# Matrix memory on one Trainium2 core: scores from stacked rounded halves, and another order of the steps of each head

## The chip, the cores and the metric

The kernel runs on one core of one Trainium2 chip. The metric is the device time of one execution in microseconds (us). Five engines work side by side, each through a list of instructions in order, and wait for each other on semaphores: TensorE (PE in the profile, its weight loads PEld), VectorE (DVE), ScalarE (ACT), GpSimd (POOL) and the DMA queue's issuer SyncE (SP).

## What is computed

The program runs three transformer layers over 512 latent and 256 context tokens of width 1024. The change lies in the second layer's mixer, a matrix memory (mLSTM) with 8 heads, keys and queries 64 wide and values 128 wide. For the last layer that needs only the latents, the reference's chunked scan equals, for each head, direction and query token t, a weighted sum over the keys s that t may see:

```python
s = jnp.einsum('bhtd,bhsd->bhts', qc, kc) * jnp.exp(logw - m_t[..., None])
num = w_inter[..., None] * jnp.einsum('bhvd,bhtd->bhtv', C, qc) + jnp.einsum('bhts,bhsv->bhtv', s, vc)
den = w_inter * jnp.einsum('bhd,bhtd->bht', n, qc) + jnp.sum(s, axis=-1)
h = num / jnp.maximum(jnp.abs(den), jnp.exp(-m_t))[..., None]
```

The forward and the backward result are added, normed over the 128 value columns (rmsnorm), multiplied by a gain and by a sigmoid gate, and go into the output projection.

## The kernel before, in words

The stage is `mlstm_stage` (lines 3052 to 3332), called once by `mix1`. It does not run the scan: it forms, for each head h and each of six 128-key blocks (`order` = 4, 5, 0, 1, 2, 3; 4 and 5 are the context), the score product of all 512 queries, and multiplies it by decay weights for both directions. The steps of a head, with their engine and line:

- **staging** (POOL, L3107): the head's 64 rows of queries are copied into one half of `qS`, the other 64 rows of which are zero, because `kT` holds two heads' keys in 128 rows. Two buffers, by parity of h.
- **spread_tops** (PE, L3120): two products put the running maxima of the two directions on all partitions of PSUM.
- **open_corners** (DVE, L3262): eight 128x128 instructions write the exponents of the diagonal blocks into `prob`.
- **weigh** 0 to 5 and **weigh_corners** (ACT, L3196, L3201): exponentials of the rest, and of the corners.
- **score** 0 to 5 (PE, L3131): one product in f32, which shows as two matmul passes. Score j waits until mix j-2 has read its PSUM bank.
- **mix** 0 to 5 (DVE, L3249): the score times the weight, for each direction, into `prob`.
- **weighted_sums** 0 to 2 (PE, L3146): 36 products in f32, two passes each (24, 30 and 18 records), of `prob` with the values and a column of ones, which gives the divisor too.
- **divisors** (DVE, L3274 to L3281), **read_first** (ACT, L3207) and **add_second** (DVE, L3287): divide and add the two directions into `hs`.
- **root** (ACT, L3214 to L3218): four sums of squares, a table load, Ln, a table load, Exp.
- **norm_heads** (DVE, L3294), **turn** (PE, L3155, four transposes), **put_out** (DVE, L3301).

The order is written by hand for each engine, as a loop over h in which three heads are in flight: head h is scored and mixed, head h-1 summed, divided and added, head h-2 normed and turned, and ACT weighs head h+1. In one turn of the loop the engines do before the change:

- PE: score 0, 1; sums 0 of h-1; score 2; sums 1 of h-1; turn h-2; score 3; spread_tops h+1; sums 2 of h-1; score 4, 5.
- ACT: weigh 0, 1 of h+1; read_first h-1; corners and weigh 2 of h+1; root h-1; weigh 3, 4, 5 of h+1.
- DVE: mix 0, 1, 2; norm h-2; mix 3; put_out h-2; open_corners h+1; mix 4, 5; divisors and add_second of h-1.
- POOL: staging, for which it waits until all scores of head h-2 are done.

The first weighted sums of a head wait for three of the four read_first of the head before (`first_read`), the others for add_second (`added`). The last head's divisors, root and norm are done by `LastHead` beside the projection that follows, and are not changed. Context for the costs: elsewhere the kernel multiplies f32 data as rounded halves of type fp32r (high, and the rest as low), one pass each.

Of the kernel before, what the change touches and what calls it, by code (L numbers as in the profile page):

```python
# [13 lines left out]
F32 = mybir.dt.float32  # L14
# [6 lines left out]
P = 128  # L21
# [103 lines left out]
class Kernel:  # L125


    def __init__(self, nc, arrays, stack):
# [66 lines left out]
        self.norm_high = sem("norm_high")  # L195
        self.norm_low = sem("norm_low")
        self.tail_lat = sem("tail_lat")
        self.last_divided = sem("last_divided")
        self.last_read = sem("last_read")
        self.last_added = sem("last_added")  # L200
# [2848 lines left out]
HEADS = 8  # L3049


def mlstm_stage(K, qT, kT, keysT, floorT, top, val, sig, yT):
# [20 lines left out]
    hs = lambda t: K.xT[:, t // 2, LAT + P * (t % 2):LAT + P * (t % 2) + P]  # L3073
    with ExitStack() as stack:
        sb = lambda name, shape: stack.enter_context(K.temp(name, shape))
        qS = sb("qS", [P, 2, LAT])
        prob = sb("prob", [P, 2, 2, 6 * LAT])
        hn, junk = sb("hn", [P, 4, P]), sb("junk", [P, P])
        den, ss = sb("den", [P, 2, 4]), sb("ss", [P, 4])
# [12 lines left out]
        @block.gpsimd  # L3092
        def _(pool):
            chain = Chain(pool, K.pool_chain)
            for half in range(2):
                r = slice(64 * half, 64 * half + 64)
                chain.step(nc.gpsimd.tensor_copy(both[r, :], K.ident[r, r]))
            chain.sync()
            for b in range(2):
                chain.step(nc.gpsimd.memset(qS[64 - 64 * b:128 - 64 * b, b, :], 0.0))  # L3100
            chain.sync()
            for h in range(HEADS):
                b, r = h % 2, slice(64 * (h % 2), 64 * (h % 2) + 64)
                if h >= 2:

                    pool.wait_ge(scored.sem, scored.base + JOBS * (h - 1))
                nc.gpsimd.tensor_copy(qS[r, b, :], qT[r, h // 2, :]).then_inc(staged.sem, 1)  # L3107
            chain.close()

        @block.tensor  # L3110
        def _(pe):
            def spread_tops(h):
                if h == 0:
                    pe.wait_ge(staged.sem, staged.base + 1)
                else:

                    pe.wait_ge(weighed.sem, weighed.base + JOBS * h)
                for d in range(2):
                    row = 32 * d + h
                    mm = nc.tensor.matmul(tops(d, 0, LAT), both[:, row:row + 1].broadcast_to([P, P]), top[:],  # L3120
                                          start=True, stop=True)
                mm.then_inc(spread.sem, 1)

            def score(h, j):
                g, s = JOBS * h + j, order[j]
                if j == 0:
                    pe.wait_ge(staged.sem, staged.base + h + 1)
                if g >= 2:

                    pe.wait_ge(mixed.sem, mixed.base + g - 1)  # L3130
                nc.tensor.matmul(scores(g), kT[:, h // 2, s * P:s * P + P], qS[:, h % 2, :],  # L3131
                                 start=True, stop=True).then_inc(scored.sem, 1)

            def weighted_sums(h, n):
                if n == 0:
                    pe.wait_ge(mixed.sem, mixed.base + JOBS * h + JOBS)
                if h > 0:

                    if n == 0:
                        pe.wait_ge(first_read.sem, first_read.base + 4 * h - 1)  # L3140
                    else:
                        pe.wait_ge(added.sem, added.base + 4 * h - (1 if n == 1 else 0))
                for d, t in (((0, 0), (0, 1), (0, 2)), ((1, 0), (1, 1), (1, 2)), ((0, 3), (1, 3)))[n]:
                    keys = [4, 5] + (list(range(t + 1)) if d == 0 else list(range(t, 4)))
                    for m, s in enumerate(keys):
                        mm = nc.tensor.matmul(K.psum[:, sums(d, t):sums(d, t) + 129], weight(h, d, s, t * P, t * P + P),  # L3146
                                              val[:, s, h, :], start=m == 0, stop=m == len(keys) - 1)
                mm.then_inc(summed.sem, 1)

            def turn(h):  # L3150
                pe.wait_ge(normed.sem, normed.base + h + 1)
                if h > 0:
                    pe.wait_ge(out_ready.sem, out_ready.base + h)
                for t in range(4):
                    mm = nc.tensor.transpose(turns[:, t * P:t * P + P], hn[:, t, :], K.ident[:])  # L3155
                mm.then_inc(turned.sem, 1)

            spread_tops(0)
            for h in range(HEADS + 1):
                now, one_back, two_back = h < HEADS, 1 <= h <= HEADS, h >= 2  # L3160
                if now:
                    score(h, 0)
                    score(h, 1)
                if h == HEADS:
                    pe.wait_ge(out_ready.sem, out_ready.base + h - 2)
                    K.keep_busy(turns, 8)
                if one_back:
                    weighted_sums(h - 1, 0)
                if now:
                    score(h, 2)  # L3170
                if one_back:
                    weighted_sums(h - 1, 1)
                if two_back:
                    turn(h - 2)
                if now:
                    score(h, 3)
                if h + 1 < HEADS:
                    spread_tops(h + 1)
                if one_back:
                    weighted_sums(h - 1, 2)  # L3180
                if now:
                    score(h, 4)
                    score(h, 5)

        @block.scalar
        def _(act):
            def weigh(h, j):
                s = order[j]
                if j == 0:

                    act.wait_ge(diag_ready.sem, diag_ready.base + h + 1)
                for d in range(2):
                    lo, hi = beyond(s, d)
                    if hi > lo:
                        col = 32 * d + h
                        op = nc.scalar.activation(weight(h, d, s, lo, hi), tops(d, lo, hi), ACT.Exp,  # L3196
                                                  bias=keysT[:, s, col:col + 1], scale=-1.0)
                op.then_inc(weighed.sem, 1)
# [4 lines left out]
            def read_first(h):  # L3203

                act.wait_ge(den_ready.sem, den_ready.base + h + 1)
                for t in range(4):
                    nc.scalar.activation(hs(t), K.psum[:, sums(0, t):sums(0, t) + P], ACT.Identity,  # L3207
                                         scale=den[:, 0, t:t + 1]).then_inc(first_read.sem, 1)

            def root(h):  # L3210
# [7 lines left out]
                nc.scalar.activation(ss[:], ss[:], ACT.Exp, scale=-0.5).then_inc(rooted.sem, 1)  # L3218
                chain.close()

            for h in range(-1, HEADS):
                ahead, back = h + 1 < HEADS, h >= 1
                if ahead:
                    weigh(h + 1, 0)
                    weigh(h + 1, 1)
                if back:
                    read_first(h - 1)
                if ahead:
                    weigh_corners(h + 1)
                    weigh(h + 1, 2)  # L3230
                if back:
                    root(h - 1)
                if ahead:
                    for j in range(3, JOBS):
                        weigh(h + 1, j)

            nc.scalar.activation(K.root[:], K.eps[:], ACT.Sqrt)

# [1 line left out]
        def _(dve):  # L3240
# [58 lines left out]
            def put_out(h):  # L3299
                dve.wait_ge(turned.sem, turned.base + h + 1)  # L3300
                nc.vector.scalar_tensor_tensor(yT[:, h, 0:LAT], turns, K.v("out_g", h), sig[:, h, :],  # L3301
                                               ALU.mult, ALU.mult).then_inc(out_ready.sem, 1)

            dve.wait_ge(K.loaded.sem, K.loaded.base + 16)
            open_corners(0)
            for h in range(HEADS + 1):
                now, one_back, two_back = h < HEADS, 1 <= h < HEADS, h >= 2
                if now:
                    mix(h, 0)
                    mix(h, 1)  # L3310
                    mix(h, 2)
                if two_back:
                    norm_heads(h - 2)
                if now:
                    mix(h, 3)
                if two_back:
                    put_out(h - 2)
                if h + 1 < HEADS:
                    open_corners(h + 1)
                if now:  # L3320
                    mix(h, 4)
                    mix(h, 5)
                if one_back:
                    divisors(h - 1)
                    add_second(h - 1)
            chain.close()
    K.loaded.base += 16
    for c, n in ((spread, HEADS), (scored, JOBS * HEADS), (summed, 3 * HEADS), (turned, HEADS - 1),
                 (weighed, JOBS * HEADS), (rooted, HEADS - 1), (first_read, 4 * HEADS - 4), (mixed, JOBS * HEADS),
                 (den_ready, HEADS - 1), (added, 4 * HEADS - 4), (normed, HEADS - 1), (diag_ready, HEADS),  # L3330
                 (out_ready, HEADS - 1), (staged, HEADS)):
        c.base += n


# [945 lines left out]
```

## Time and profile before

| | us |
|---|---|
| median of 3 runs | 2786.57 (2785.32 to 2791.9) |
| the profiled execution's own time | 2783.43 |
| its span in the trace | 2781.7 |
| busy in the span: PE, PEld | 2661.6, 2163.9 |
| busy in the span: DVE, ACT, POOL | 1515.0, 914.2, 285.5 |

The span goes from the first to the last instruction. Times of a row are in us from the start of the span unless marked ns. A row of the timeline merges neighbouring instructions of one kind: start, time from the first start to the last end, engine, line, operation, output and inputs, shape and count, and in brackets how long the engine was idle before and whose signal ended that. The end of an instruction overlaps the start of the next by a pipeline's depth, so the cost of one in a row of many is the distance of the starts. The stage of the change lies between 1360.5 and 1501.3 us.

### The profile page before, as it was taken

Reading aid. Unit: us, or ns where it says so; the run is one execution under the profiler, and the core shown is the slowest. Engines: PE = TensorE matmul, PEld = TensorE weight load, DVE = VectorE, ACT = ScalarE, POOL = GpSimd, SP = SyncE. Lnnn points to the kernel's source line nnn. Section 1 sums busy time; section 2 is a strip of 40 time slices with the busy share of each in tenths; the row PEclk is TensorE's granted clock in tenths of the full one; section 3 lists DMA queues with packets and bytes.
Section 4 is the critical chain, followed back from the end, with each engine's and each line's share of the span. In section 5 each row is a group of like instructions: output and inputs, shape, how many; then the busy total and the mean of one; then the engine's idle time right before and its main releaser. Section 6 shows DMA issues by size and latency. Waiting matters only on the chain. (4 is left out here: it accounts for less than half of the span.)

```text
span 2781.7 us, 32433 instructions
## 1 busy us (share of the span) xinstructions
PE 2661.6 (96%) x13424; PEld 2163.9 (78%) x13424; DVE 1515.0 (54%) x2047; ACT 914.2 (33%) x1222; POOL 285.5 (10%) x161
## 2 busy tenths in 40 slices
PE   7998999999999999999889999999999899999998
PEld 5876666688888888888767888888686678888887
DVE  6326899874329536571366543444789833433332
ACT  4332434423212212352265331332323622332221
POOL 2111223000000000000000000000240644000000
PEclk9999999999999999999999999999999999999999
DMA  7011001331125324122001222223120222222221
GB/s 273 25 51 54 31 31 46 145 136 68 62 75 204 144 79 171 46 93 89 18 1 46 83 80 102 106 73 110 61 86 14 77 105 91 76 97 93 106 82 62
DMA packets 37037, 236.10 MB, mean 85 GB/s; under 512 B 4128, under 2 KB 5152, under 8 KB 13216
## 3 DMA queue, kind: packets, MB, share of 16 engines
q1 hardware_dynamic: 36896, 234.11, 23.4%
q8 instruction: 103, 1.69, 0.2%
q14 instruction: 38, 0.31, 0.0%
HBM read 231.99 MB, written 2.10 MB: 84 GB/s over the span
## 5 line engine op out<-in xcount | busy, mean ns | idle before, releaser
L369 PE MATMUL pair<-h_high,w_high 128*128 128x512 f32 x1984 | 714.4, 369 | 10.2 <-DVEq L1239 4.9
L370 PE MATMUL pair<-h_low,w_high 128*128 128x512 f32 x1984 | 710.1, 366 | 0.0
L375 PE MATMUL pair<-h_high,w_low 128*128 128x512 f32 x1984 | 444.4, 366 | 0.8 <-POOL w_low L323 0.8
L323 DVE TENSOR_TENSOR w_low<-ring,w_high 128x2048 fp32r<-128x2048 f32 (+5 forms) x164 | 342.1, 2091 | 186.4 <-ACT w_high L301 178.9
L369 PEld LDWEIGHTS pair<-h_high,w_high 128*128 128x128 f32 x1984 | 374.1, 189 | 76.2 <-issue 7.3
L370 PEld LDWEIGHTS pair<-h_low,w_high 128*128 128x128 f32 x1984 | 374.3, 189 | 64.0 <-issue 1.4
L375 PEld LDWEIGHTS pair<-h_high,w_low 128*128 128x128 f32 x1984 | 346.1, 189 | 63.0 <-POOL w_low L323 1.2
L301 ACT ACTIVATE w_high<-ring 128x2048 fp32r<-128x2048 f32 (+4 forms) x166 | 288.1, 1736 | 309.4 <-PE pair L375 203.9
L369 PE MATMUL pair<-high,w_high 128*128 128x512 f32 (+1 forms) x704 | 249.1, 363 | 1.0 <-DVE low L1283 1.0
L370 PE MATMUL pair<-low,w_high 128*128 128x512 f32 (+1 forms) x704 | 249.0, 363 | 0.0
L1275 DVE TENSOR_TENSOR gate<-gate,pair 128x512 f32<-128x512 f32 (+1 forms) x66 | 51.2, 776 | 239.0 <-PE pair L375 230.1
L311 POOL CAST w_high<-ring 128x1024 fp32r<-128x1024 f32 x25 | 30.5, 1249 | 1299.3 <-DVE coef L724 706.1
L375 PE MATMUL pair<-high,w_low 128*128 128x512 f32 (+1 forms) x704 | 153.8, 363 | 0.0
L369 PEld LDWEIGHTS pair<-high,w_high 128*128 128x128 f32 x704 | 132.8, 189 | 22.8 <-DVE low L1283 2.1
L370 PEld LDWEIGHTS pair<-low,w_high 128*128 128x128 f32 x704 | 132.9, 189 | 20.8
L375 PEld LDWEIGHTS pair<-high,w_low 128*128 128x128 f32 x704 | 122.0, 189 | 20.6
L1224 ACT ACTIVATE high<-gate 128x512 fp32r<-128x512 f32 (+2 forms) x66 | 46.4, 704 | 277.7 <-DVE gate L1275 277.7
L323 POOL TENSOR_TENSOR w_low<-ring,w_high 128x2048 fp32r<-128x2048 f32 x21 | 97.1, 4624 | 111.0 <-ACT w_high L301 110.4
L2097 ACT ACTIVATE prob<-pair 128x512 f32<-128x512 f32 x112 | 65.0, 594 | 122.8 <-PE pair L2038 122.6
L2051 PE MATMUL pair<-prob,val 128*128 128x512 f32 x192 | 99.1, 598 | 0.0
L1111 DVE SCALAR_TENSOR_TENSOR xT<-pair,mod,xT 128x512 f32<-128x512 f32 (+1 forms) x48 | 27.5, 613 | 106.9 <-PE pair L375 106.9
L1215 ACT ACTIVATE gate<-pair,vec 128x768 f32<-128x768 f32 (+1 forms) x44 | 38.9, 884 | 132.6 <-PE pair L375 119.5
(464 smaller groups left out, 4011.4 us busy)
## 6 DMA issues: line engine op xcount, KB each, us to landing
ring<-in_w_up SPq DMA_DIRECT2D x66, 1024.0 KB, 4.8
ring<-in_w_ada SPq DMA_DIRECT2D x32, 1024.0 KB, 4.8
ring<-in_w_down SPq DMA_DIRECT2D x32, 704.0 KB, 4.0
ring<-in_w_ada0r SPq DMA_DIRECT2D x16, 1024.0 KB, 4.8
ring<-in_w_merge_b SPq DMA_DIRECT2D x14, 1024.0 KB, 4.8
ring<-in_w_down SPq DMA_DIRECT2D x8, 1024.0 KB, 4.7
ring<-in_w_att_in SPq DMA_DIRECT2D x6, 1024.0 KB, 5.2
ring<-in_w_heads SPq DMA_DIRECT2D x6, 1024.0 KB, 5.0
```

Of the source, the lines that this page charges most:

```text
L301: self.nc.scalar.activation(self.w_high[:, n % 2, 0:floats], self.ring[:, chunk % RING, 0:floats], ACT.Copy).then_inc(self.high_ready.sem, 1)
L311: return engine.tensor_copy(to, of)
L323: (on or self.nc.vector).tensor_tensor(self.w_low[:, n % 2, 0:floats], self.ring[:, chunk % RING, 0:floats], self.w_high[:, n % 2, 0:float ...
L369: self.nc.tensor.matmul(out[:, a:e], w_high[:, k, at], high[:, k, a:e], start=k == 0, stop=False)
L370: self.nc.tensor.matmul(out[:, a:e], w_high[:, k, at], low[:, k, a:e], start=False, stop=False)
L375: mm = self.nc.tensor.matmul(out[:, a:e], w_low[:, k, at], high[:, k, a:e], start=False, stop=k == kt - 1)
L1111: op = nc.vector.scalar_tensor_tensor(x, self.out(b)[:, a:e], K.mod[:, self.gate * KD + b, a // LAT:a // LAT + 1], x, ALU.mult, ALU.add)
L1215: nc.scalar.activation(g, ps[:, 0:tokens], ACT.Identity, bias=bias, scale=middle).then_inc(tap_ready.sem, 1)
L1224: nc.scalar.activation(one(high[:, bass.ds(i * RING + s, 1), 0:tokens]), g, ACT.Copy).then_inc(high_done.sem, 1)
L1275: nc.vector.tensor_tensor(g[:, 0:tokens], g[:, 0:tokens], K.pairs[2 * (s % 2) + 1][:, 0:tokens], ALU.mult).then_inc(hidden_ready.sem, 1)
L2051: mm = nc.tensor.matmul(out_lat(u), values(u, s), prob[:, g % 3, :], start=s == 0, stop=s == 5)
L2097: nc.scalar.activation(prob[:, g % 3, :], scores(g), ACT.Exp).then_inc(exped.sem, 1)
```

## The change

1. **Scores.** `kS` holds, for each parity, the rounded (fp32r) keys of the head in its own 64 rows and the rest, keys minus rounded keys, in the other 64; `qS` holds the rounded queries in both halves; `qL` the rest of the queries. A score is then two fp32r products: `kS` with `qS` over 128 rows, and the head's rows of `kS` with `qL` over 64. The product of the two rests is left out. (`qS` in the other half is written from `qT` and rounded on the way.)
2. **Staging.** POOL does five operations a head in place of one (three copies, two subtractions). Head 0 is staged by ACT (two copies) and DVE (one copy, two subtractions), ahead of their loops; PE's first score waits for that. The two memsets go.
3. **Order.** PE: scores 4 and 5 stand ahead of sums 2 of h-1. ACT: read_first h-1 stands first, then weigh 0 and 1, corners, weigh 2 to 5 of h+1, and root h-1 last. DVE: after put_out come mix 4, 5, divisors h-1, then open_corners h+1, then add_second h-1.

```diff
@@ staging
-        qS = sb("qS", [P, 2, LAT])
+        half = lambda name, shape: stack.enter_context(K.temp(name, shape, F32R))
+        kS, qS, qL = half("kS", [P, 2, ALL]), half("qS", [P, 2, LAT]), half("qL", [P, LAT])
+        own = lambda h: slice(64 * (h % 2), 64 * (h % 2) + 64)
+        other = lambda h: own(h + 1)
...
-            for half in range(2):
-                r = slice(64 * half, 64 * half + 64)
-                chain.step(nc.gpsimd.tensor_copy(both[r, :], K.ident[r, r]))
-            chain.sync()
-            for b in range(2):
-                chain.step(nc.gpsimd.memset(qS[64 - 64 * b:128 - 64 * b, b, :], 0.0))
-            chain.sync()
-            for h in range(HEADS):
-                b, r = h % 2, slice(64 * (h % 2), 64 * (h % 2) + 64)
+            nc.gpsimd.tensor_copy(both[0:64, :], K.ident[0:64, 0:64])
+            nc.gpsimd.tensor_copy(both[64:P, :], K.ident[64:P, 64:P]).then_inc(staged.sem, 1)
+            for h in range(1, HEADS):
+                b, r, o = h % 2, own(h), other(h)
                 if h >= 2:
                     pool.wait_ge(scored.sem, scored.base + JOBS * (h - 1))
-                nc.gpsimd.tensor_copy(qS[r, b, :], qT[r, h // 2, :]).then_inc(staged.sem, 1)
+                chain.step(nc.gpsimd.tensor_copy(qS[r, b, :], qT[r, h // 2, :]))
+                chain.step(nc.gpsimd.tensor_copy(kS[r, b, :], kT[r, h // 2, :]))
+                nc.gpsimd.tensor_copy(qS[o, b, :], qT[r, h // 2, :])
+                chain.sync()
+                nc.gpsimd.tensor_tensor(qL[r, :], qT[r, h // 2, :], qS[r, b, :].bitcast(F32), ALU.subtract)
+                nc.gpsimd.tensor_tensor(kS[o, b, :], kT[r, h // 2, :], kS[r, b, :].bitcast(F32),
+                                        ALU.subtract).then_inc(staged.sem, 1)
@@ score, and the loop of TensorE
-                if j == 0:
+                if j == 0 and h == 0:
+                    pe.wait_ge(K.head_low.sem, K.head_low.base + 1)
+                elif j == 0:
                     pe.wait_ge(staged.sem, staged.base + h + 1)
...
-                nc.tensor.matmul(scores(g), kT[:, h // 2, s * P:s * P + P], qS[:, h % 2, :],
-                                 start=True, stop=True).then_inc(scored.sem, 1)
+                b, keys = h % 2, slice(s * P, s * P + P)
+                nc.tensor.matmul(scores(g), kS[:, b, keys], qS[:, b, :], start=True, stop=False)
+                nc.tensor.matmul(scores(g), kS[own(h), b, keys], qL[own(h), :],
+                                 start=False, stop=True).then_inc(scored.sem, 1)
...
-                if one_back:
-                    weighted_sums(h - 1, 2)
                 if now:
                     score(h, 4)
                     score(h, 5)
+                if one_back:
+                    weighted_sums(h - 1, 2)
@@ ScalarE
+            nc.scalar.activation(qS[own(0), 0, :], qT[own(0), 0, :], ACT.Copy).then_inc(K.head_high.sem, 1)
+            nc.scalar.activation(kS[own(0), 0, :], kT[own(0), 0, :], ACT.Copy).then_inc(K.head_high.sem, 1)
             for h in range(-1, HEADS):
                 ahead, back = h + 1 < HEADS, h >= 1
+                if back:
+                    read_first(h - 1)
                 if ahead:
                     weigh(h + 1, 0)
                     weigh(h + 1, 1)
-                if back:
-                    read_first(h - 1)
-                if ahead:
                     weigh_corners(h + 1)
-                    weigh(h + 1, 2)
+                    for j in range(2, JOBS):
+                        weigh(h + 1, j)
                 if back:
                     root(h - 1)
-                if ahead:
-                    for j in range(3, JOBS):
-                        weigh(h + 1, j)
@@ VectorE
+            r, o = own(0), other(0)
+            dve.wait_ge(K.head_high.sem, K.head_high.base + 1)
+            nc.vector.tensor_copy(qS[o, 0, :], qT[r, 0, :])
+            nc.vector.tensor_tensor(qL[r, :], qT[r, 0, :], qS[r, 0, :].bitcast(F32), ALU.subtract)
+            dve.wait_ge(K.head_high.sem, K.head_high.base + 2)
+            nc.vector.tensor_tensor(kS[o, 0, :], kT[r, 0, :], kS[r, 0, :].bitcast(F32),
+                                    ALU.subtract).then_inc(K.head_low.sem, 1)
...
-                if h + 1 < HEADS:
-                    open_corners(h + 1)
                 if now:
                     mix(h, 4)
                     mix(h, 5)
                 if one_back:
                     divisors(h - 1)
+                if h + 1 < HEADS:
+                    open_corners(h + 1)
+                if one_back:
                     add_second(h - 1)
```

## Rows read from the trace of the kernel before

**Rows 1.** The page's first part: busy time of each engine over the whole span.
```profile
PE 2661.6 (96%) x13424; PEld 2163.9 (78%) x13424; DVE 1515.0 (54%) x2047; ACT 914.2 (33%) x1222; POOL 285.5 (10%) x161
```

**Rows 2.** Windows: stretch, length, busy PE, PEld, DVE, ACT, POOL, granted clock, DMA.
```profile
1360.00:1362.00 2.00, 0.00 (x0) 0.00 (x0) 0.20 (x1) 1.28 (x1) 1.34 (x4) 1.00 0.24 61
...
1363.20:1366.50 3.30, 3.30 (x6) 1.32 (x4) 2.16 (x8) 0.28 (x1) 0.31 (x1) 0.50 0.00 0
1366.60:1369.90 3.30, 1.37 (x3) 0.30 (x2) 2.30 (x4) 3.30 (x6) 0.00 (x0) 1.00 0.00 0
...
1374.00:1490.00 116.00, 102.95 (x632) 77.07 (x631) 74.08 (x207) 72.42 (x173) 3.66 (x6) 1.00 0.00 1
```

**Rows 3.** Timeline of TensorE in one turn (h = 5) of the loop.
```profile
1444.02 2.92 PE L3146 MATMUL pair<-val,prob 128*128 128x129 f32 x24 [0.47 <-ACT xT L3207]
...
1447.64 3.51 PE L3146 MATMUL pair<-val,prob 128*128 128x129 f32 x30
...
1451.54 1.02 PE L3131 MATMUL pair<-qS,kT 128*128 128x512 f32 x2
...
1452.87 2.17 PE L3146 MATMUL pair<-val,prob 128*128 128x129 f32 x18
```

**Rows 4.** Timeline of VectorE in the same turn.
```profile
1442.16 0.22 DVE L3274 SCALAR_TENSOR_TENSOR den<-pair,floorT 128x6 f32<-128x6 f32 x2
...
1442.68 0.20 DVE L3281 RECIPROCAL den<-den 128x8 f32<-128x8 f32 x1
...
1450.30 0.69 DVE L3294 TENSOR_TENSOR hn<-xT,ss 128x512 f32<-128x512 f32 x1 [1.58 <-ACT ss L3218]
1452.60 0.89 DVE L3249 SCALAR_TENSOR_TENSOR prob<-pair,prob 128x384 f32<-128x384 f32 x2 [1.61 <-PE pair L3131]
1453.41 0.74 DVE L3301 SCALAR_TENSOR_TENSOR yT<-pair,vec,sig 128x512 f32<-128x512 f32 x1
1455.16 2.16 DVE L3262 SCALAR_TENSOR_TENSOR prob<-pair,keysT,causal 128x128 f32<-128x128 f32 x8 [1.01 <-PE pair L3146]
1457.24 1.67 DVE L3249 SCALAR_TENSOR_TENSOR prob<-pair,prob 128x256 f32<-128x256 f32 x4
```

**Rows 5.** Timeline of ScalarE in the same turn, up to the next one's first weighing.
```profile
1440.69 2.42 ACT L3196 ACTIVATE prob<-pair,keysT 128x512 f32<-128x512 f32 x4 [5.37 <-DVE prob L3262]
1442.98 1.15 ACT L3207 ACTIVATE xT<-pair,den 128x128 f32<-128x128 f32 x4
1443.98 1.10 ACT L3201 ACTIVATE prob<-prob 128x1024 f32<-128x1024 f32 x1
...
1445.39 0.36 ACT L3214 ACTIVATE junk<-xT 128x128 f32<-128x128 f32 x1
...
1447.16 1.28 ACT L3216 ACT_TABLE_LOAD   x1
...
1450.18 1.81 ACT L3196 ACTIVATE prob<-pair,keysT 128x256 f32<-128x256 f32 x5
1457.35 2.42 ACT L3196 ACTIVATE prob<-pair,keysT 128x512 f32<-128x512 f32 x4 [5.37 <-DVE prob L3262]
```

**Rows 6.** Timeline of TensorE: two fp32r products, one after the other.
```profile
1503.31 0.39 PE L1375 MATMUL pair<-h_low,w_high 128*128 128x512 f32 x1
...
1503.54 0.40 PE L1375 MATMUL pair<-h_high,w_high 128*128 128x512 f32 x1
```

**Rows 7.** Timeline around 2284, VectorE then GpSimd, and one GpSimd line's durations (ns min/median/max).
```profile
2284.24 4.23 DVE L3936 TENSOR_TENSOR cc<-cc,hd 128x512 f32<-128x512 f32 x1
...
2283.28 4.64 POOL L323 TENSOR_TENSOR w_low<-ring,w_high 128x2048 fp32r<-128x2048 f32 x1 [6.62 <-ACT w_high L301]
...
L2206 POOL TENSOR_TENSOR c_low<-xT,c_high x8: 1812/1831/2808, 275.7 to 374.3; 64x768 fp32r<-64x768 f32 x8
```

**Rows 8.** Timeline of the stage's first corners and of its last sums.
```profile
1364.03 2.16 DVE L3262 SCALAR_TENSOR_TENSOR prob<-pair,keysT,causal 128x128 f32<-128x128 f32 x8 [3.83 <-PE pair L3120]
...
1498.80 2.17 PE L3146 MATMUL pair<-val,prob 128*128 128x129 f32 x18
```

More of the change, by code:

```diff
@@ L197, in __init__ @@
         self.tail_lat = sem("tail_lat")
+        self.head_high = sem("head_high")
+        self.head_low = sem("head_low")
         self.last_divided = sem("last_divided")
@@ L3330, in mlstm_stage @@
                  (den_ready, HEADS - 1), (added, 4 * HEADS - 4), (normed, HEADS - 1), (diag_ready, HEADS),
-                 (out_ready, HEADS - 1), (staged, HEADS)):
+                 (out_ready, HEADS - 1), (staged, HEADS), (K.head_high, 2), (K.head_low, 1)):
         c.base += n
```

## The prediction, made before the changed kernel was run

> **What bounds the kernel now.** The page puts TensorE at 2661.6 of 2781.7 us busy [rows 1], so I first asked whether the stage of the change is bound by it as well. The windows say: 102.95 of 116 us busy between 1374 and 1490, at a granted clock of 1.00 [rows 2]. That leaves over a tenth idle, so work taken from TensorE is not simply time saved. I therefore followed one turn of the loop (h = 5) through the timelines, and every wait in it. ScalarE's first weighings of two turns start at 1440.69 and 1457.35 [rows 5]: a turn takes 16.66 us. Two closed chains compete for that.
>
> *Chain A, through the sums.* Sums 0 start at 1444.02 when ScalarE's read_first is done; sums 1 and 2 follow with scores and transposes between them, and what waits for the end of sums 2 is open_corners, at 1455.16 [rows 3, 4]. Corners take 2.16, ScalarE then weighs for 2.29 (1440.69 to 1442.98) and reads for some 1.0 before the next sums 0 [rows 5]: 11.14 + 2.19 + 2.29 + 1.04 = 16.66. This chain binds.
>
> *Chain B, through the root.* ScalarE: weigh 2.29, read 1.00, corners and weigh 2 1.41, then the root; norm_heads starts at 1450.30, so the root costs 1450.30 - 1445.39 = 4.91 [rows 4, 5]. Then norm 0.69, transposes and start of score 3 0.55 (1450.99 to 1451.54), score 3 until mix 3 1.06, mix 3 0.81, put_out 0.74, after which VectorE stood 1.01 idle for sums 2 [rows 3, 4], then corners 2.16 + 0.03. Without that idle time the chain is 15.65 us. So chain B has 1.0 us of slack, no more. What is to be seen: norm_heads of head h-2 stands before mix 3 of head h in VectorE's list, so all that stands behind it waits for ScalarE's root.
>
> **Part 1, the scores.** An f32 score is two passes, 1.02 us to its end [rows 3]; two fp32r products follow each other at 0.23 and the last ends 0.40 after its start [rows 6]. A score costs TensorE 0.46 for some 0.86, 2.4 us per head. On chain B only score 3 counts: 1.06 becomes 0.23 + 0.40 + 0.04 = 0.67. That the second product has 64 rows is taken to gain nothing; a gain would be at most 0.23.
>
> **Part 2, staging.** GpSimd's dearest step is a 64x768 subtraction, 1.83 us median [rows 7]; five steps of at most that are under 9.2 us, my estimate is 5.2. It starts when head h-2 is scored and is due a whole turn later: hidden by head h-1's turn of 16.7 us, costed at nothing. Were that cover gone, the whole 5.2 would stand ahead of each head's score 0. Beside it VectorE does instructions with one operand in PSUM, for which I take nothing.
> At the head of the stage it does matter. VectorE must copy and subtract twice after ScalarE's first copy, about 0.6 + 0.7 + 1.0 from 1361.1 on (a 128x512 instruction of this kind takes 0.69, [rows 4]): first corners at 1363.4, where they were at 1364.03 [rows 8]. But GpSimd stages head 1 in that time, and a VectorE tensor_tensor on 128x512 took 4.23 us when a GpSimd subtraction had started 0.96 before it, ending 0.55 after that one [rows 7]. If both subtractions are held until GpSimd's chain of 5.2 is through, corners start at 1367.4. I take 1364.8, nearer to the lower end since most of GpSimd's steps there are short.
> The Trainium skill (GPSIMD Engine Reference, Key points) says that the two engines share their SBUF interfaces and contend when the VectorE instruction has two SBUF inputs. The trace agrees; by the rule alone the start is late, without it 0.6 us early.
>
> **Part 3, the order.** Chain A: scores 4 and 5 come ahead of sums 2, read_first no longer waits for corners and weighings. It becomes sums 0 2.76, score 2 0.46, sums 1 3.4, transposes 0.4, score 3, spread, scores 4 and 5 1.84, sums 2 2.29, divisors 0.72, three reads 0.95 [rows 3 to 6]: 12.8 us. It would bind no more.
> Chain B, from the moment R when a root is done: norm 0.69 and 0.55 as before, 0.67, so mix 3 starts at R+1.91 and ends its share at 2.72. Now put_out (0.74), mix 4 and 5 (about 1.6) stand ahead of the divisors: 5.05. On TensorE score 5 waits for mix 3 (2.85 with the signal), ends at 3.3, and sums 2, now behind it, take 2.29 from 3.35: 5.65. So the divisors start at 5.65, end 0.72 later (1442.16 to 1442.88), corners run from 6.45 to 8.61, weigh starts at R+8.65. ScalarE had nothing to do meanwhile but the read. Then weigh 0, 1 2.29, corners and weigh 2 1.41, weigh 3 to 5 some 1.64 (the row's 1.81 less the overlap), which used to come behind the root, and the root 4.91: 10.25 [rows 4, 5]. **Turn: 18.9 us**, where it was 16.66. Of the terms, the moved weighings give +1.64, mix 4 and 5, sums 2 and divisors ahead of corners +1.95, the read -1.00, the score -0.39. There are five such turns from the root of head 0 to that of head 5: +11.2.
> Start: head 0 has its own path. spread of head 1 waits for all of head 0's weighings (corners 2.16 + 5.34 after the first corners), and score 4 stands behind it, then mix 4 and 5, then corners of head 1; walked through by the same durations the first root is done 37.8 after the first corners, before 36.3 (1364.03 to 1400.3). +1.5, and +0.8 for the later corners: +2.3, between +0.9 and +4.9.
> Tail: from the root of head 5 (1483.6) to the last sums' end (1500.97, [rows 8]) it was 17.3. Now divisors end at 6.37, three reads at 7.2, sums 0 and 1 to 13.5, transposes and sums 2 16.1: -1.2.
>
> **The clock.** In the new turn TensorE is done with sums 1 at about R+15.1 (read 7.3, sums 0, score 2 behind mix 0 at 11.2, sums 1) and goes on at R+19.6: 4.5 us idle. In this trace the clock was 0.50 in 1363.2 to 1366.5, right after some 3 us of idleness (nothing in 1360 to 1362), again after a stretch with 1.37 of 3.3 us busy, and 1.00 all through the loop, where the longest pauses are 1.5 [rows 2]. So I expect the lower level, 1.2 GHz, once per head, over a stretch like those of the rows, most of it behind the pause. Then transposes (+0.4) and score 3 (+0.6) double and spread and score 4 keep score 5 back: +1.1 per turn and in the tail. Bounds: nothing, and +2.0 where it reaches into sums 2. 5.5 and 1.1.
> The Trainium skill (TensorE: Matmul & The Clock Gate, Why this matters for your kernels) warns of idle gaps between bursts of matmuls, as they bring the low rate back. That speaks against this change; without the rule its turn is 18.9, with it 20.
>
> **Sum.** 2.3 + 11.2 + 5.5 - 0.1 = +18.9, against the profiled execution's 2783.43: 2802.3. That execution lies 3.1 below the median of the runs, 2786.57, so the median forecast is 2805.
>
> **Rivals.** (a) *The clock holds at 2.4 GHz.* The pause falls where it does no harm, as the loop's 1.5 us pauses do now. 2.3 + 11.2 - 1.2 = +12.3: 2799. For: it has held for 116 us. Against: the new pause is three times as long.
> (b) *The clock falls for longer*, +2.0 a turn, and staging holds VectorE at the start: 4.9 + 11.2 + 10 + 0.8 = +27: 2813.
> (c) *Faster: the root stays off the path*, its place being VectorE's norm_heads. Chain A then sets the turn, 12.8, or ScalarE's own list, 11.3: 3.8 x 5 = -19, with start and tail -18: 2769. It decides when the chain through the root falls under 16.66, 2.2 us shorter than I make it. For: TensorE is the busiest engine and loses 2.4 us per head. Against: VectorE already idles 1.58 for the root [rows 4] though it comes earlier in ScalarE's list now.
> (d) *No difference.* The two table loads of the root (1.28 each, [rows 5]) disappear in the new order: turn 16.3, sum near -0.7: 2786. Against: Exp, Ln, Exp still alternate.
>
> **Chances.** Forecast 0.48, (a) 0.20, (b) 0.15, (c) 0.08, (d) 0.09. The range 2795 to 2814 holds the first three, with the bounds of the start. A measurement of this kernel can tell about 0.3%, 8.4 us, from no change: all of the first three are beyond it, so slower 0.83, same 0.09, faster 0.08.
>
> **What would show it.** First weighings of successive turns 19 to 20 us apart; VectorE's idle time before norm_heads up from 1.58 to some 5, ended by ScalarE's Exp; ScalarE idle some 7 between a root's end and the first weighing, the read within; TensorE idle some 4 before the transposes; score passes 0.23 apart; granted clock under 1.00 in the loop. I am wrong if turns are shorter than 16.7, if the wait before norm_heads is no longer than now, or if GpSimd's staging ends a wait of TensorE in the loop.

## The result, and the profile after

The changed kernel takes 2828.41 us (median of 4 runs, 2828.31 to 2829.63), the kernel before 2786.31 in the runs beside it: 1.0156 times as long, 95% interval 1.0144 to 1.0168. The profiled execution of after has a span of 2827.9 us, 46.2 more than before. The forecast was 2805 in a range of 2795 to 2814. The kernel did become slower, as forecast, but by 42.1 us where the sum had 18.9.

Nearly all of it lies in the stage of the change, which ends at 1545.8 us (GpSimd's first instruction of the next stage), before at 1501.3. By VectorE's norm_heads the 44.6 us divide like this: head 0's norm comes 7.0 later (1407.27 for 1400.31), the five turns from head 0's to head 5's take 34.4 more (117.7 for 83.3), the tail 3.2 more.

Timeline of VectorE in one turn of the kernel after; it answers to [rows 4]; the last row but one is ScalarE's first weighing. L3305 is norm_heads, L3260 the mixes, L3312 put_out, L3285 to L3292 the divisors, L3273 the corners.

```profile
1454.90 0.69 DVE L3305 TENSOR_TENSOR hn<-xT,ss 128x512 f32<-128x512 f32 x1 [5.48 <-ACT ss L3230]
1457.40 0.89 DVE L3260 SCALAR_TENSOR_TENSOR prob<-pair,prob 128x384 f32<-128x384 f32 x2 [1.82 <-PE pair L3143]
1458.21 0.74 DVE L3312 SCALAR_TENSOR_TENSOR yT<-pair,vec,sig 128x512 f32<-128x512 f32 x1
1459.70 0.89 DVE L3260 SCALAR_TENSOR_TENSOR prob<-pair,prob 128x256 f32<-128x256 f32 x2 [0.75 <-PE pair L3143]
1461.15 0.89 DVE L3260 SCALAR_TENSOR_TENSOR prob<-pair,prob 128x128 f32<-128x128 f32 x2 [0.56 <-PE pair L3143]
1465.32 0.23 DVE L3285 SCALAR_TENSOR_TENSOR den<-pair,floorT 128x6 f32<-128x6 f32 x2 [3.28 <-PE pair L3158]
...
1466.09 2.16 DVE L3273 SCALAR_TENSOR_TENSOR prob<-pair,keysT,causal 128x128 f32<-128x128 f32 x8
1468.29 2.42 ACT L3208 ACTIVATE prob<-pair,keysT 128x512 f32<-128x512 f32 x4 [1.05 <-DVE prob L3273]
...
1478.60 0.69 DVE L3305 TENSOR_TENSOR hn<-xT,ss 128x512 f32<-128x512 f32 x1 [5.48 <-ACT ss L3230]
```

The turn is 23.70 us. The idle time before norm_heads has gone from 1.58 to 5.48, as forecast. Count from the root's end, R = 1454.90. ScalarE's half of the circle is as predicted: its first weighing starts at 1468.29 and the next norm 10.31 later, where the sum had 10.25. The other half, R to that weighing, takes 13.39 where the sum had 8.65, or 9.75 with the 1.1 for the clock. What is late is TensorE each time: mix 3 comes at R+2.5, mix 4 and 5 wait for scores 4 and 5 (0.75, 0.56), and the divisors start at R+10.4, after VectorE stood 3.28 us idle for the last sums.

Timeline of TensorE in the same turn; it answers to [rows 3]. L3142 and L3143 are the two products of a score, L3158 the sums.

```profile
1455.64 0.66 PE L3167 MATMUL pair<-ident,hn 128*128 128x128 f32 x4 [3.87 <-DVE hn L3305]
1456.06 0.59 PE L3142 MATMUL pair<-qS,kS 128*128 128x512 f32 x1
...
1459.60 0.79 PE L3142 MATMUL pair<-qS,kS 128*128 128x512 f32 x1
1460.32 0.79 PE L3143 MATMUL pair<-qL,kS 64*128 64x512 f32 x1
1461.05 4.24 PE L3158 MATMUL pair<-val,prob 128*128 128x129 f32 x18
...
1471.01 0.50 PE L3142 MATMUL pair<-qS,kS 128*128 128x512 f32 x1 [0.80 <-DVE prob L3260]
1471.44 0.50 PE L3143 MATMUL pair<-qL,kS 64*128 64x512 f32 x1
1471.87 3.62 PE L3158 MATMUL pair<-val,prob 128*128 128x129 f32 x30
```

Two things are to be seen. The steps of a score (from the start of one product to the start of the next) are 0.43 us (1471.01, 1471.44, 1471.87), not the 0.23 of [rows 6]; a score of two such steps is as dear as the f32 one. And at low clock (granted 0.50) they are 0.72 (1459.60, 1460.32), and the low clock reaches through the last sums, 4.24 us for 2.17 before. The windows show how long a low stretch lasts (first row, two turns earlier) and the pause ahead of the transposes of the turn just walked through (second row):

```profile
1409.00:1418.50 9.50, 9.50 (x28) 6.41 (x27) 3.92 (x12) 0.00 (x0) 4.62 (x5) 0.50 0.00 0
...
1452.00:1455.60 3.60, 0.00 (x0) 0.00 (x0) 0.69 (x1) 2.82 (x4) 0.00 (x0) 1.00 0.00 0
```

TensorE was busy all through 1409.0 to 1418.5 and its clock stayed at 0.50, 1.2 GHz, behind a pause like that of the second row. In full, each low stretch of the loop is 10.2 us but one of 6.8. Before, the one in [rows 2] was some 3.3 us. So two questions were open: how much of the loss is the order, and why the scores are neither cheap nor bring the clock back.

### The profile page after: what moved, and what is told of

Its sections match the earlier page's. It is cut to its first block and busy times, and to the rows that moved or that the text cites. A ratio compares the mean times of both kernels' runs of the same rounds, so it can differ in the third digit from the quotient of the medians.

```text
span 2827.9 us, 32457 instructions
## 1 busy us (share of the span) xinstructions
PE 2689.8 (95%) x13424; PEld 2184.5 (77%) x13424; DVE 1519.7 (54%) x2050; ACT 916.5 (32%) x1224; POOL 316.2 (11%) x186
## 5 line engine op out<-in xcount | busy, mean ns | idle before, releaser
L371 PE MATMUL pair<-h_high,w_high 128*128 128x512 f32 x1984 | 714.3, 369 | 10.2 <-DVEq L1241 4.9
L372 PEld LDWEIGHTS pair<-low,w_high 128*128 128x128 f32 x704 | 132.9, 189 | 20.8
L3158 PEld LDWEIGHTS pair<-val,prob 128*128 128x128 f32 x576 | 78.4, 221 | 7.8 <-issue 7.8
```

What stands on the lines that cost most here:

```text
L371: self.nc.tensor.matmul(out[:, a:e], w_high[:, k, at], high[:, k, a:e], start=k == 0, stop=False)
L372: self.nc.tensor.matmul(out[:, a:e], w_high[:, k, at], low[:, k, a:e], start=False, stop=False)
```

## The experiments

Each ran beside the kernel before. A turn is the distance of two norm_heads between head 0 and head 5 (where single turns differ, the usual one stands there; after has one of 22.7, order_only one of 22.5, full_rows one of 20.8); the clock is the mean granted between 1405 and 1475 us. The filler is explained below.

| run | scores | order | us | ratio to before (95%) | turn | clock |
|---|---|---|---|---|---|---|
| before | f32 | old | 2785 | 1 | 16.7 | 1.00 |
| after | 128 + 64 rows | new | 2828.4 | 1.0156 (1.0144 to 1.0168) | 23.7 | 0.78 |
| scores_only | 128 + 64 rows | old | 2801.5 | 1.0058 (1.0041 to 1.0075) | 18.4, 19.1 | 0.86 |
| order_only | f32 | new | 2816.4 | 1.0115 (1.0098 to 1.0132) | 21.4 | 0.88 |
| full_rows | 128 + 128 | new | 2808.2 | 1.0081 (1.0064 to 1.0098) | 20.1 | 0.91 |
| filled | 128 + 64, filler | new | 2804.9 | 1.0070 (1.0053 to 1.0087) | 19.8 | 1.00 |
| full_filled | 128 + 128, filler | new | 2794.8 | 1.0037 (1.0023 to 1.0052) | 18.9 | 1.00 |
| scores_full_old_order | 128 + 128 | old | 2789.7 | 1.0015 (1.0006 to 1.0025) | 17.2 to 17.8 | 0.88 |
| f32_half_rows | f32, 64 rows | old | 2809.2 | 1.0085 (1.0069 to 1.0102) | 18.8 to 20.1 | 0.88 |
| full_filled_root_early | 128 + 128, filler | root before weigh 3 | 2791.3 | 1.0026 (1.0016 to 1.0036) | 18.0 | 1.00 |
| norm_late | 128 + 128 | norm late | 2770.4 | 0.9951 (0.9935 to 0.9968) | 14.2 | 1.00 |
| norm_late_f32 | f32 | norm late | 2778.2 | 0.9978 (0.9969 to 0.9988) | 15.4 | 1.00 |
| norm_late_64 | 128 + 64 | norm late | 2781.6 | 0.9989 (0.9980 to 0.9999) | 15.4 | 1.00 |

### Each half alone

**scores_only**: the change with the loops of the three engines as before.

> The stacked fp32r scores and their staging, with all three orders as before the change. Theory A (the second product's 64-row weights are not loaded ahead, so a score is two steps of 0.43 us, as dear as the f32 one): turns of 16.7 us as before, TensorE steps of 0.43 in the scores, 2786 within 4 us. Theory B (the scores are cheap, 0.23 a step, and only the order hurts): a turn loses 0.8 us in the sums' chain, 15.9, and the time is near 2781.

Neither. The steps are 0.43, as A has it, but the time is 16 us up, outside both theories. The clock falls in a loop whose longest pause of TensorE is 1.7 us, where before it is 1.5. The first sums of a turn, and the window of a turn:

```profile
1453.39 5.50 PE L3158 MATMUL pair<-val,prob 128*128 128x129 f32 x24 [0.64 <-ACT xT L3219]
...
1441.50:1460.60 19.10, 16.75 (x91) 13.44 (x90) 10.87 (x31) 12.07 (x31) 5.07 (x5) 0.82 0.00 0
```

The first sums take 5.50 us for 2.92 [rows 3]. Staging is no cause: TensorE waits only for VectorE and ScalarE in the loop.

**order_only**: the three moves put into the kernel before.

> The three new orders with the f32 scores and staging of before. Theory A (the order makes a closed chain through the root, and the pause in it costs TensorE its clock): turns of 21 to 23 us, VectorE idle some 5 before norm_heads, granted clock 0.50 after the pause, but back sooner than with fp32r scores; 2811 to 2821. Theory B (the order costs little and the stacked scores, cold, cost the time): turns under 17.5 us, 2787 to 2792.

A holds: the turn is 21.4, VectorE's idle time before norm_heads 5.49, the time 2816.4. The order alone makes the kernel slower. Its pause ahead of the transposes is that of after, 3.87, but its low stretches are 3.4 us, two of them 6.8, where those of after are 10.2. TensorE's transposes, and the two windows behind them:

```profile
1446.81 1.12 PE L3155 MATMUL pair<-ident,hn 128*128 128x128 f32 x4 [3.87 <-DVE hn L3291]
```
```profile
1446.30:1449.60 3.30, 2.79 (x7) 1.76 (x8) 0.45 (x1) 0.00 (x0) 0.00 (x0) 0.50 0.01 2
1449.80:1466.00 16.20, 13.20 (x84) 10.06 (x82) 10.25 (x30) 10.10 (x26) 0.61 (x1) 1.00 0.00 0
```

### Why a score is not cheap

**full_rows**: the second product over all 128 rows, the head's 64 and 64 of zeros; `causal`, `junk` and `hn` lie in free columns of `xT` to make room.

```diff
+            chain.step(nc.gpsimd.memset(qL[other(0), 0, :].bitcast(F32), 0.0))
+            chain.step(nc.gpsimd.memset(qL[other(1), 1, :].bitcast(F32), 0.0))
...
-                nc.tensor.matmul(scores(g), kS[own(h), b, keys], qL[own(h), :],
+                nc.tensor.matmul(scores(g), kS[:, b, keys], qL[:, b, :],
```

> The change with the second product over all 128 rows (the rest of the queries with zeros in the other head's rows, so the result is the same; three small tiles lie elsewhere to make room). Theory A (weights of 64 rows behind weights of 128 are not loaded ahead): steps of 0.23 us at full clock, the score 0.4 us shorter, TensorE busier after the pause and its clock back sooner; turns near 21, 2808 to 2815. Theory B (what spaces the products is something else, as the accumulation or the signals): steps stay at 0.43 (0.72 at half clock), 2826 to 2830.

A holds, with turns a little under its 21 and the time at its lower end. Timeline of TensorE and of its weight loads (PEld) in the run full_filled, where the clock is full; then the second load of after; then the windows of full_rows behind the pause:

```profile
1440.47 0.39 PE L3145 MATMUL pair<-qS,kS 128*128 128x512 f32 x1
1440.47 0.19 PEld L3146 LDWEIGHTS pair<-qL,kS 128*128 128x128 f32 x1
1440.70 0.40 PE L3146 MATMUL pair<-qL,kS 128*128 128x512 f32 x1
```
```profile
1471.44 0.18 PEld L3143 LDWEIGHTS pair<-qL,kS 64*128 64x128 f32 x1 [0.25 <-issue]
```
```profile
1444.80:1448.00 3.20, 3.20 (x10) 2.53 (x9) 2.41 (x6) 0.00 (x0) 0.00 (x0) 0.50 0.00 0
1448.50:1465.00 16.50, 10.38 (x81) 9.37 (x80) 8.31 (x25) 11.25 (x27) 4.61 (x5) 1.00 0.00 0
```

The load for the second 128-row product starts at 1440.47, 0.23 ahead of that product; the load of the 64-row one in after starts at 1471.44, together with its product. So the steps are 0.23, a low stretch is 3.4 us (one is 6.8) in place of 10.2, and the turns are 20.1 us: with more rows to multiply the kernel is 20 us faster. That turn is the 20.0 of the forecast.

**f32_half_rows**: the kernel before, its f32 scores over the head's 64 rows.

```diff
+                own = slice(64 * (h % 2), 64 * (h % 2) + 64)
-                nc.tensor.matmul(scores(g), kT[:, h // 2, s * P:s * P + P], qS[:, h % 2, :],
+                nc.tensor.matmul(scores(g), kT[own, h // 2, s * P:s * P + P], qS[own, h % 2, :],
```

> The kernel before, with its f32 scores taken over the head's own 64 rows only (the same sum, the other rows being zeros). Theory A (weights of another row count are not loaded ahead of the matmuls before them, so each pass waits for its own load): steps of some 0.6 us where they were 0.43, turns longer by about 1 us in the chain, and the clock perhaps falling; 2792 to 2802. Theory B (it is special to fp32r, or to two row counts within one sum): steps stay at 0.43 and the time at 2786.

Mixed. The time went up by more than A said, but not by the steps at full clock: behind other 64-row passes one starts after 0.43, as with 128 rows; only at the change from and to 128-row products is a step some 0.1 longer (0.53). So the cost lies where the row count changes, not at each 64-row load. The larger loss comes with the clock. The window of a turn, before and in this run:

```profile
1441.50:1458.20 16.70, 14.69 (x90) 10.99 (x90) 11.00 (x32) 11.18 (x28) 0.61 (x1) 1.00 0.00 0
```
```profile
1424.65:1444.52 19.87, 18.56 (x91) 12.73 (x90) 10.88 (x32) 12.46 (x32) 0.61 (x1) 0.83 0.00 0
```

The same passes of the same columns, over half the rows, and the granted clock is 0.83 where it was 1.00; the longest pause is 1.31, no longer than the 1.50 of before. Whether it is the rows themselves or the longer steps at the changes that lower the clock, no run separates.

**scores_full_old_order**: full_rows with the old loops.

> The stacked scores over 128 rows with the three orders of before. Theory A (only 64-row products cost the clock in the old order): clock 1.00, a turn loses two times 0.4 us in the chain through the sums, 15.9 us; 2780 to 2784. Theory B (fp32r scores as such leave TensorE too little to do in the old order): the clock falls in the loop as in the run with the 64-row product, turns of 17.5 or more, 2792 or more.

B, in a milder form: the clock falls for 3.4 to 6.8 us a turn, the turns are 17.8 to 17.2 rather than 15.9, and the time is 2789.7, under B's 2792 but 0.15% above before. TensorE's longest pause is 2.29 now, for 1.50 before, and it is busy for 14.11 of 17.4 us. That the cheaper scores cost the clock through this idle time is likely but not shown: this order was not run with a filler.

### The clock and the chain

**filled**: `keep_busy` gives TensorE 16 products of ones, whose result nobody reads. They stand in `turn`, ahead of its wait for the norm, and fill the pause.

```diff
+                if h < HEADS - 2:
+                    K.keep_busy(turns, 16)
                 pe.wait_ge(normed.sem, normed.base + h + 1)
```

> The change with 16 idle products of ones (32 passes of 128 columns, some 3.7 us) on TensorE in the pause ahead of the transposes, for all heads but the last. Theory A (half of the loss is the clock): granted clock 1.00 from the second turn on, turns of 19.5 to 20 us, 2803 to 2808. Theory B (the low clock is a sign and not a cause, the chain waits for other engines): turns stay at 23.7 and the time at 2828.

A holds, at 19.76 a turn: the clock costs 3.9 us of after's turn. Work that computes nothing saves 23.5 us.

**full_filled**: both, the 128-row product and the filler.

> Both cures together: the second product over 128 rows, and 16 idle products in the pause ahead of the transposes. Theory A (the prediction's chain through the root is right and only the price of the 64-row product was wrong): granted clock 1.00 in the loop and turns of 18.9 us, the sum's figure for a clock that holds; 2801 to 2804. Theory B (the order costs less than the chain says, and the rest was clock): turns under 18 us, below 2797.

The turn is A's to the hundredth, though the time came 6 us under its range. That range took only the turns from after's time; in the profiles, head 0's part is also 5.4 us shorter than in after and the tail 4.4 (see the start and the tail below). Timeline of VectorE:

```profile
1438.29 0.69 DVE L3310 TENSOR_TENSOR xT<-xT,ss 128x512 f32<-128x512 f32 x1 [5.47 <-ACT ss L3235]
1440.20 0.89 DVE L3265 SCALAR_TENSOR_TENSOR prob<-pair,prob 128x384 f32<-128x384 f32 x2 [1.22 <-PE pair L3146]
...
1443.92 0.23 DVE L3290 SCALAR_TENSOR_TENSOR den<-pair,floorT 128x6 f32<-128x6 f32 x2 [0.59 <-PE pair L3161]
...
1457.19 0.69 DVE L3310 TENSOR_TENSOR xT<-xT,ss 128x512 f32<-128x512 f32 x1 [5.48 <-ACT ss L3235]
```

Mix 3 at R+1.91, divisors at R+5.63, turn 18.90: the sum had 1.91, 5.65 and 18.9.

**full_filled_root_early**: the same with `root(h - 1)` between weigh 2 and weigh 3, where it was before the change.

> The run full_filled with the root back ahead of weigh 3 to 5. Theory A (each step between the corners and the root lies on the one closed chain): the three weighings, 1.64 us, leave it, turns of 17.3 us for 18.9, 8 us less over five turns, 2785 to 2789. Theory B (another chain binds as soon as this one is shorter, or the weighings come too late for mix 3): turns of 18.3 or more, 2791 or more.

The turn is 18.0, between the two, the time at B's edge, and the rows say why. TensorE's:

```profile
1431.96 3.74 PE L416 MATMUL pair<-ones 128*128 128x128 f32 x32
1435.53 0.60 PE L3172 MATMUL pair<-ident,xT 128*128 128x128 f32 x4
```

The norm was done at 1434.6, but behind the filler, sized for the longer pause, the transposes started only at 1435.5: that took 0.9 us of the gain. VectorE's idle time before the norm fell by 1.71 (5.47 to 3.76). That the chain itself became shorter by the full 1.64 is worked out from this, not shown by a turn.

### The root off the path

**norm_late**: full_rows (no filler) with the norm just ahead of the divisors.

```diff
@@ VectorE
                     mix(h, 2)
-                if two_back:
-                    norm_heads(h - 2)
-                if now:
                     mix(h, 3)
-                if two_back:
-                    put_out(h - 2)
                 if now:
                     mix(h, 4)
                     mix(h, 5)
+                if two_back:
+                    norm_heads(h - 2)
                 if one_back:
                     divisors(h - 1)
                 if h + 1 < HEADS:
                     open_corners(h + 1)
+                if two_back:
+                    put_out(h - 2)
                 if one_back:
                     add_second(h - 1)
@@ TensorE
-                if two_back:
+                if two_back and not now:
                     turn(h - 2)
...
                     weighted_sums(h - 1, 2)
+                if two_back and now:
+                    turn(h - 2)
```

> The change with 128-row products, and norm_heads moved behind mix 5, right ahead of the divisors, put_out behind the corners and the transposes behind the last sums. Theory A (the loss in the order is that mixes and last sums wait for the root; nothing else in it is bad): the chain through the root becomes norm 0.7, divisors 0.7, corners 2.2, ScalarE 10.25 = 13.9 us a turn, clock 1.00, 2770 to 2776, faster than both. Theory B (put_out and transposes late, or another wait, take its place): turns over 15 us, 2778 or more.

A holds: turns of 14.2 (13.9 by the sum), clock 1.00, and the kernel is faster than before and after. Timeline of VectorE:

```profile
1443.09 0.84 DVE L3310 TENSOR_TENSOR xT<-xT,ss 128x512 f32<-128x512 f32 x1 [0.23 <-ACT ss L3235]
1443.98 0.23 DVE L3290 SCALAR_TENSOR_TENSOR den<-pair,floorT 128x6 f32<-128x6 f32 x2
...
1454.44 2.62 DVE L3265 SCALAR_TENSOR_TENSOR prob<-pair,prob 128x384 f32<-128x384 f32 x6 [2.65 <-PE pair L3146]
1457.25 0.69 DVE L3310 TENSOR_TENSOR xT<-xT,ss 128x512 f32<-128x512 f32 x1 [0.19 <-ACT ss L3235]
```

The root still releases the norm, but VectorE idles 0.2 us for it instead of 5.5, because mixes 3 to 5 are now done in the meantime.

**norm_late_again**: the same kernel, measured five more times.

> The run norm_late once more, in five rounds, for its ratio: 0.995 of the time before, within 0.0015, if that result was no accident of the day; over 0.998 if it was.

2771.06 us, ratio 0.9947, interval 0.9934 to 0.9961: it holds.

**norm_late_f32**: norm_late's order in the kernel before. **norm_late_64**: in the change as it is.

> The order of the run norm_late with the f32 scores and staging of before. Theory A (the gain of that run is the order's, and stacked scores add little while the chain through the root binds): only the passes behind the root's chain are dearer, turns of 14.2 to 15 us, clock 1.00, 2766 to 2776. Theory B (the order needs the cheaper scores): turns of 16 us or more, 2780 or more.

> The order of norm_late with the stacked scores as the change has them, the second product over 64 rows. Theory A (64 rows cost both the step, 0.43 for 0.23, and the clock): the clock falls in the loop, turns of 16 to 18 us, 2782 to 2795. Theory B (the clock fell only because of the pauses of the other orders): turns as in norm_late, near 14.5, under 2776.

With f32 scores the turn is 15.4 and the time 2778.2, a little over A's ranges and 0.2% under before: the order alone gains, and the 128-row scores take 1.2 us a turn more off. With 64 rows the turn is 15.4 too and A's clock is wrong: in the loop it holds at 1.00, with TensorE's pauses at 1.0 us or a little more. The time, 2781.6, lies between the two theories. So 64-row products do not lower the clock everywhere. They did in the loops with longest pauses of 1.3, 1.7 and 3.9 us; where the border lies, and whether the pauses decide it, these runs do not show. What is left here is their longer steps. The window of a turn of norm_late_64:

```profile
1436.40:1451.80 15.40, 14.37 (x93) 11.09 (x92) 11.39 (x33) 11.27 (x27) 5.42 (x6) 1.00 0.00 0
```

## Why the prediction was wrong, point by point

**The order (Part 3): right.** Mixes, last sums and divisors did come to stand on one closed chain with the root. The sum gave 18.9 us for a turn with a full clock; full_filled measured 18.90, with its inner points within 0.02. The waits it named (norm_heads 5.5, the transposes 3.9) are there.

**The scores (Part 1): the step that failed.** "That the second product has 64 rows is taken to gain nothing": it has no gain, but it has a cost, which the sum left out. Priced at 0.23 a step from 128-row products [rows 6], it took 0.43, so a score did not become 0.4 us cheaper. By filled against full_filled, both at full clock, this is 19.76 - 18.90 = 0.86 a turn. Those rows were the wrong witness: both of their products have 128 rows.

**The clock: right in kind, too small in size, and for the same reason.** The low stretch was forecast like those of before, for +1.1 a turn. With 128-row products that is so: 20.14 - 18.90 = 1.24. With the change's products it lasts up to 10.2 us and costs 23.7 - 19.8 = 3.9; in it a 64-row step is 0.72 for 0.43, too. The bound of +2.0 was too small. So of the 3.7 us a turn that the forecast of 20.0 missed, 0.9 is the step and 2.7 the clock (1.24 to 3.9); full_rows, which undoes just this, has the forecast's turn, and its time of 2808.2 lies in the range.

**The start: too low, by the same step.** Forecast +2.3, measured +7.0. The corners start at 1364.73, as taken (1364.8); VectorE's subtraction of 64x512 took 1.21 there beside GpSimd's copies. But the clock stayed at 0.50 from 1364 to 1384, and head 0's scores and first sums ran at half speed:

```profile
1370.00:1374.00 4.00, 4.00 (x7) 1.69 (x6) 2.57 (x6) 2.48 (x7) 0.00 (x0) 0.50 0.00 0
1374.00:1384.00 10.00, 10.00 (x30) 6.82 (x30) 6.33 (x16) 4.61 (x10) 5.06 (x5) 0.50 0.00 1
```

The profiled executions enter this stage at times up to 3.6 us apart, so heads of the stage are better compared from the start of TensorE's last product of the stage before. From there the first norm comes after 40.9 us in before, 47.5 in after and 42.2 in full_rows. With 128 rows the start costs +1.3, even less than forecast.

**The tail**: -0.1 forecast, +3.2 measured; scores and last sums of the last turns ran at low clock again. In full_rows it is -0.1. So with 128-row products start, turns and tail come to +1.3, +18.1 and -0.1, together 19.3 for the sum's 18.9. The 1.0 that the start came in lower and the 1.4 that the turns came in higher partly cancel there.

**Staging (Part 2) in the loop: right**, 5.2 us estimated, 5.1 to 5.3 a head measured, hidden. Rival (b) had the sign of the error, a longer low clock, but not its reason, and its 2813 was still too low. Rivals (a), (c) and (d) did not happen; something like (c), 2769, came only when norm_heads was moved (2770.4).

## What to carry to other kernels

When instructions of three heads are interleaved by hand, close the circle before moving one: follow each wait back to the same step one turn earlier and sum it. A step whose result is needed late (here the root) belongs in the waiting engine's list as late as its buffers allow, not in front of work that does not need it. And a product over fewer rows, between products over 128, was not a cheaper one here: try to pad it to the row count of its neighbours, and take its price from a row of the same shape in the same company.

## What the runs showed of the hardware

- An fp32r product of 512 columns over 64 rows between products over 128 starts 0.43 us after the one before it, and so does the next; with 128 rows it is 0.23. The 64-row load starts together with its product (1471.44), the 128-row load one step ahead (1440.47 for 1440.70). At low clock the steps are 0.72 and 0.43. The differences, 0.20 and 0.29, are about a weight load (0.19 and 0.29).
- The granted clock stayed at 0.50 for 9.5 us in which TensorE was never idle, while it ran 64-row scores and the last sums. With 128-row scores in the same order it came back after 3.4 us, in one turn after 6.8. f32 passes over 64 rows went with a clock of 0.83 in a turn in which the same passes over 128 rows had 1.00. I had not expected rows to matter; by which property they do stays open.
- Cheaper work for TensorE need not save time: in the old order 128-row scores are 0.4 us cheaper each, the clock is 0.88 for 1.00, and the kernel is 0.15% slower.
